# Attention in a two-layer hybrid block: maxima streamed one pair per step in fp16, sums by full-width matmuls, shift rows by DMA

## The reference

```python
s = jnp.einsum('bqhgd,bkhd->bhgqk', qi, k, preferred_element_type=F32) * scale
p = jax.nn.softmax(s, axis=-1).astype(v.dtype)
return jnp.einsum('bhgqk,bkhv->bqhgv', p, v)
```

## Time and profile before

| what | value |
|---|---|
| time, median of 3 runs | 4570.11 us (4565.5 to 4571.17) |
| time of the profiled execution | 4556.52 us, span 4554.7 us |
| TensorE busy | 3887.8 us, 85% of the span |
| VectorE, ScalarE, GpSimd busy | 2159.6, 1203.1, 798.9 us |
| maxima, VectorE L1465 | 600 instructions, 336.5 us busy, 327.8 us idle ahead of them |
| GpSimd adds L1414 and L1409 | 219 instructions, 450.6 and 63.4 us |

### The profile page before, as it was taken

How to read it: one execution, slowest core, us unless ns; L and a number is a source line. 1 busy time by engine, 2 the same in 40 slices (tenths; PEclk the granted TensorE clock), 3 DMA queues, 4 the chain that set the end, 5 groups by cost and what they waited for, 6 DMA issues and landing times. The chain is left out here.

```text
span 4554.7 us, 49366 instructions
## 1 busy us (share of the span) xinstructions
PE 3887.8 (85%) x20550; PEld 2092.8 (46%) x20550; DVE 2159.6 (47%) x3601; ACT 1203.1 (26%) x1589; POOL 798.9 (18%) x412
## 2 busy tenths in 40 slices
PE   6698459689989799999996696478799985999996
PEld 6455337323345555555553454455233332444443
DVE  1782886554530623333335683854555316333334
ACT  0321333223331321111112321332233323221211
POOL 0000641056650000000000000700277600000000
PEclk7898665689999799999998897755799997999998
DMA  4210013010002221111101210031100021111110
GB/s 167 54 38 4 1 44 116 17 35 9 1 3 81 74 65 42 42 39 40 42 28 37 56 41 1 1 123 54 30 8 1 1 74 46 51 51 51 51 47 37
DMA packets 207632, 194.37 MB, mean 43 GB/s; under 512 B 9719, under 2 KB 174386, under 8 KB 206770
## 3 DMA queue, kind: packets, MB, share of 16 engines
q1 hardware_dynamic: 203250, 182.84, 12.9%
q10 hardware_dynamic: 4160, 8.39, 0.5%
HBM read 167.48 MB, written 14.68 MB: 40 GB/s over the span
## 5 line engine op out<-in xcount | busy, mean ns | idle before, releaser
L324 PE MATMUL mlp_acc<-hh,mlp_w 128*128 128x512 f16 (+1 forms) x3840 | 752.8, 359 | 49.9 <-DVE mlp_w L314 49.9
L324 PE MATMUL mlp_acc<-mlp_aa,mlp_w 128*128 128x512 f16 (+1 forms) x3840 | 749.2, 358 | 0.0
L324 PEld LDWEIGHTS mlp_acc<-hh,mlp_w 128*128 128x128 f16 x3840 | 376.5, 98 | 424.3 <-DVE mlp_w L314 50.8
L324 PEld LDWEIGHTS mlp_acc<-mlp_aa,mlp_w 128*128 128x128 f16 x3840 | 375.8, 98 | 371.1
L1465 DVE TENSOR_REDUCE at_mx<-at_small 128x1 f32<-128x512 f32 (+1 forms) x600 | 336.5, 591 | 327.8 <-PE at_small L1511 197.1
L1414 POOL TENSOR_TENSOR at_accp<-at_accp,at_p 128x1024 f32<-128x1024 f32 x192 | 450.6, 2347 | 151.7 <-ACT at_p L1445 150.5
L324 PE MATMUL in_acc<-hh,in_w 128*128 128x512 f16 (+1 forms) x2088 | 400.2, 354 | 71.0 <-DVE in_w L314 58.5
L1445 ACT ACTIVATE at_p<-at_sT 128x1024 f32<-128x1024 f32 x246 | 252.1, 1025 | 475.9 <-PE at_sT L1556 458.3
L647 DVE SCALAR_TENSOR_TENSOR yf<-mlp_acc,yf 128x1280 f32<-128x1280 f32 (+1 forms) x112 | 152.0, 1357 | 398.6 <-PE mlp_acc L324 398.6
L324 PEld LDWEIGHTS in_acc<-hh,in_w 128*128 128x128 f16 (+1 forms) x2088 | 208.0, 100 | 261.3 <-DVE in_w L314 59.3
L634 DVE TENSOR_TENSOR mlp_r<-mlp_r 128x1280 f32<-128x1280 f32 (+1 forms) x64 | 86.9, 1358 | 476.2 <-ACT mlp_r L615 476.2
(11 more groups left out here) (268 smaller groups left out, 4870.2 us busy)
## 6 DMA issues: line engine op xcount, KB each, us to landing
mlp_stage<-in_w_ff SPq DMA_DIRECT2D x128, 512.0 KB, 3.9
pa_wada<-in_w_ada SPq DMA_DIRECT2D x16, 2048.0 KB, 8.2
in_stage<-in_w_in SPq DMA_DIRECT2D x36, 512.0 KB, 4.2
set_wada<-in_w_ada ACTq DMA_DIRECT2D x4, 2048.0 KB, 20.2
out_stage<-in_w_out SPq DMA_DIRECT2D x16, 512.0 KB, 5.0
nf_wada<-in_w_ada SPq DMA_DIRECT2D x4, 2048.0 KB, 8.7
x<-x_scratch SPq DMA_DIRECT2D x1, 5120.0 KB, 16.0
xin<-in_x SPq DMA_DIRECT2D x8, 512.0 KB, 6.1
```

The source lines that it names most:

```text
L324: last = self.nc.tensor.matmul(acc[0:mw, a:a + c], w[:, wh, k, m0:m0 + mw], src[:, sh, k0 + k, a:a + c], start=(k == 0 and wh == 0 and sh ...
```

## The change

MSHIFT is gone. Six things change:

- `plan()` spreads the maxima: one pair of tasks a step, ending LEAD=4 steps before their unit. The last chunk of 256 keys is taken for two query tiles in one task, so a long unit has 20 max tasks, all 512 wide; a short one has 4. They and the row task are all ahead of the values product.
- VectorE writes the maxima over chunks as fp16 into `top`; no negation follows.
- row: one fp16 product of `top` (8 columns) with an fp16 identity, which VectorE makes at the start. ScalarE copies 8x128 with scale -1 into `row`, and SyncE sends it by DMA into the queries, two DMAs for a long unit and four for a short one, behind the loads of the first three pairs of heads in its list.
- sum: two fp32 products, 64 columns of ones as the weights and 512 columns of `accp` moving, behind the values product. All 64 partitions of a par get the sum. ScalarE copies the 128x512 into `o32`.
- VectorE takes the reciprocal of `o32` itself, four pieces of 128x128, one a step, 5 to 8 steps after the unit's last, and the product with `acc` at 9. Where a short unit follows, all is done at step 4 after the last.
- PRING is 5, not 4. The bc task is gone.

```diff
-PRING = 4
+PRING = 5
+LEAD = 4
 def maxes(u):
+        if not units[u].long:
+            return [("max", u, par, 0, (q, q + 1)) for q in (0, 2) for par in range(2)]
+        whole = [("max", u, par, c, (q,)) for q in range(4) for c in range(2) for par in range(2)]
+        return whole + [("max", u, par, 2, (q, q + 1)) for q in (0, 2) for par in range(2)]
 def plan():
+        both = [(u, k) for u in range(1, U) for k in range(len(maxes(u)) // 2)]
+        when = {}
+        for n in range(len(both) - 1, -1, -1):
+            u, k = both[n]
+            when[n] = min(base[u] - LEAD, when.get(n + 1, N) - (1 if n + 1 < len(both) else 0))
+        for n, (u, k) in enumerate(both):
+            want.setdefault(max(when[n], n // 2), []).extend(maxes(u)[2 * k:2 * k + 2])
+        for u in range(1, U):
+            want.setdefault(base[u] - LEAD + 1, []).append(("row", u))
         for u in range(U):
             end = base[u + 1] - 1
             soon = u + 1 < U and not units[u + 1].long
+            sum_at[u] = min(end + (3 if soon else 4), N)
+            want.setdefault(sum_at[u], []).append(("sum", u))
+            for k in range(4):
+                piece_at.setdefault(min(end + (4 if soon else 5 + k), N), []).append((u, k))
+            scale_at[u] = min(end + (4 if soon else 9), N)
 # SyncE
+                for pr in range(QRING):
+                    load(pr)
+                for u in range(U):
+                    sp.wait_ge(s_row, u + 1)
+                    for par in range(2):
+                        for pr, tok, c, n in units[u].parts:
+                            r = 4 * par + c // P
+                            dst = shift_row(pr, par)[:, tok:tok + n]
+                            sp.dma_start(dst, row[r:r + n // P, u % 2, :]).then_inc(s_shift[u % 2], 16)
 # ScalarE
-                                nc.scalar.activation(row[:, tok:tok + n], sm[j % 2][R:R + 1, c:c + n], ACT.Copy)\
+                            nc.scalar.activation(row[:, u % 2, :], sm[j % 2][0:8, 0:P], ACT.Copy, scale=-1.0).then_inc(s_row, 1)
+                            nc.scalar.activation(o32[:, u % 2, :], sm[j % 2][:, :], ACT.Copy).then_inc(s_sums, 1)
 # VectorE
-                                ch(nc.vector.reduce_max(neg[:, u, :, :], mx[:, u, :, :, 0:len(cks)], AX.X))
-                                nc.vector.tensor_scalar(neg[:, u, :, :], neg[:, u, :, :], -1.0, MSHIFT,
+                                nc.vector.reduce_max(top[:, u, :].rearrange("p (a q) -> p a q", a=2),
+                                                     mx[:, u, :, :, 0:len(units[u].keys)], AX.X).then_inc(s_top, 1)
+                        part = o32[:, u % 2, k * P:(k + 1) * P]
+                        pieces[u] = ch(nc.vector.reciprocal(part, part))
 # TensorE
-                                last = nc.tensor.matmul(out[R:R + 1, q * P:(q + 1) * P], neg[:, u, par, q:q + 1],
+                            last = nc.tensor.matmul(out[0:8, 0:P], top[:, u, :], ident[:, :], start=True, stop=True)
-                                                            accp[:, u % 2, par, q * P:(q + 1) * P], e.ones[:, 0:1],
+                                last = nc.tensor.matmul(out[64 * par:64 * par + 64, :], e.ones[:, 0:64],
+                                                        accp[:, u % 2, par, :], start=True, stop=True)
-                                                            rc[:, u % 2, 4 * par + q:4 * par + q + 1].broadcast_to([P, 64]),
                     scores(i)
-                    tasks(i, slice(0, EARLY))
+                    tasks(i, ahead)
                     if i >= LAG:
                         weighted(i - LAG)
-                    tasks(i, slice(EARLY, None))
+                    tasks(i, ("sum",))
```

More of the change, by code:

```diff
@@ L1203 @@
 LAG = 2
-EARLY = 2
-PRING = 4
+PRING = 5
+LEAD = 4
 QRING = 3
@@ L1260, in maxes @@
     def maxes(u):
-        return [("max", u, par, q, c) for q in range(4) for c in range(len(units[u].keys)) for par in range(2)]
+        if not units[u].long:
+            return [("max", u, par, 0, (q, q + 1)) for q in (0, 2) for par in range(2)]
+        whole = [("max", u, par, c, (q,)) for q in range(4) for c in range(2) for par in range(2)]
+        return whole + [("max", u, par, 2, (q, q + 1)) for q in (0, 2) for par in range(2)]
+    sum_at, piece_at, scale_at = {}, {}, {}
     def plan():
         want = {}
[L1265 to L1273, removed]
+        for t in maxes(0) + [("row", 0)]:
+            want.setdefault(-1, []).append(t)
+        both = [(u, k) for u in range(1, U) for k in range(len(maxes(u)) // 2)]
[7 more added lines that the diff above has]
+            want.setdefault(base[u] - LEAD + 1, []).append(("row", u))
         for u in range(U):
@@ L1276, in plan @@
             soon = u + 1 < U and not units[u + 1].long
[L1277 to L1280, removed]
+            sum_at[u] = min(end + (3 if soon else 4), N)
[3 more added lines that the diff above has]
+            scale_at[u] = min(end + (4 if soon else 9), N)
         for i in sorted(want):
             for t in want[i]:
-                put(min(i, N), t)
+                put(i, t)
     plan()
@@ L1324, in attention, with shifts @@
                 last_max[t[1]] = kinds[:j + 1].count("max")
-            elif t[0] == "row":
-                rows_at[j] = sum(len(units[w[1]].parts) for w in small[:j + 1] if w[0] == "row")
-                rows_through[t[1]] = rows_at[j]
+        def shifts(u):
+            return sum(16 * 2 * len(units[v].parts) for v in range(u % 2, u + 1, 2))
         def hi_of(t, q):
@@ L1376, in place, with load @@
                     sp.dma_start(to, src).then_inc(signal, 16)
-                for pr in range(4):
+                def load(pr):
                     if pr % 2 == 0:
@@ new lines, in tasks @@
+                            for n, q in enumerate(tiles):
+                                pr, tok = units[u].tile(q)
+                                if pr < 4 and pr % 2 == 0 and pr not in loaded:
+                                    pe.wait_ge(s_kload[pr // 2], 16 * 6)
+                                    loaded.add(pr)
+                                if pr < 4:
+                                    R = slice(64 * par, 64 * par + 64)
+                                    query, key = hi_of(f.aq[R, pr, :], tok), kk[R, pr // 2, a:a + w]
+                                else:
+                                    b = 2 * (pr - 4) + par
+                                    query, key = f.qb[0:96, 0, b, tok:tok + P], f.kb[0:96, 0, b, a:a + w]
+                                last = nc.tensor.matmul(out[:, n * w:(n + 1) * w], query, key, start=True, stop=True)
+                        elif kind == "row":
+                            pe.wait_ge(s_top, u + 1)
+                            if u == 0:
+                                pe.wait_ge(s_id, 1)
+                            last = nc.tensor.matmul(out[0:8, 0:P], top[:, u, :], ident[:, :], start=True, stop=True)
+                        else:
@@ L1546, in scores @@
                     if s == 0:
-                        pe.wait_ge(s_row, rows_through[u])
+                        pe.wait_ge(s_shift[u % 2], shifts(u))
+                        for pr, _, _, _ in units[u].parts:
+                            if pr < 4 and (pr, "q") not in loaded:
+                                pe.wait_ge(s_load[pr % QRING], per_pair * (pr // QRING + 1))
+                                loaded.add((pr, "q"))
                     if i >= 2:
```

117 lines of the change are left out of this document (45 added, 72 removed).

## The result

| | before | after |
|---|---|---|
| median of 4 runs each on one chip | 4570.64 us (4565.5 to 4576.94) | 4463.71 us (4456.26 to 4468.1) |
| ratio, 95% interval | | 0.9764 (0.9745 to 0.9783) |
| profiled execution: time, span | 4556.52, 4554.7 us | 4466.4, 4464.6 us |

The forecast was 4484 with a range of 4445 to 4530. In the profiled pair the gain is 90.1 us. Counted from the first load of keys to the end of GpSimd's last low half, attention takes 753.8 us in place of 855.3: 101.5 less. The code outside attention, which is the same, takes 11.4 us more. For that reason I compare kernels by their medians and, for sizes, by their attention alone.

A forecast was written before the change was run, and what follows sets the result against it. TensorE's list was taken to bound the kernel. Loops of 353.3 us (from 399.1) and 325.1 (from 374.3) gave -95.0; starts +8.7 and -1.2, ends +2: -85.5, so 4484 against the median; range 4445 to 4530.

The forecast's parts named there:

- What bounds it: Both attention stretches: TensorE's list, busy in 99%, sets the pace; GpSimd's adds start every 2.42 us and stay under it.
- A step with a pair of maxima: TensorE in attention: a pair adds 0.32 us to a bare 1.98 in group A, 0.43 to 2.42 in group B.
- The sum: Two full-width fp32 products on TensorE, once a unit: 1.12 us, being 1.02 and 0.1 for the change of tasks.
- The row: Row's fp16 product on TensorE, mostly waiting for a max's bank: 1.3 us a unit in group A, 0.8 in B.
- The long waits: Layer 0, long units behind short ones: the values product waits 3.7 us for acc's bank; two of them, 7.4.
- The start at the lower clock: Start of each layer's attention loop: 5 us for running at the lower clock, as before.
- The first row: Start of attention: row DMAs behind SyncE's loads delay the first scores by 8.7 us in layer 0; -1.2 in layer 1.
- The tails: Ends of the layers: bare reciprocal pieces against the sums and spreads they replace, +2 us for both layers.
- The waits are hidden: Rival: waits for row and acc hidden, group A's unit 24.3 us in place of 25.5; 4452 us, chance 0.17.
- The clock falls still: Rival: waits of the new order make the clock fall, 28 us of the saving come back; 4512 us, chance 0.13.
- Rows late: Rival: the row's DMA lands 3 to 4 us later, 25 unit starts wait 1 to 2 each; 4522 us, chance 0.06.
- The reciprocals shut out: Rival: VectorE's reciprocal pieces wait for GpSimd's adds; 4682 us, chance 0.05, or 4566 with 1 us waits, chance 0.05.

The follow-up runs named there:

- e4: Changed kernel with PRING 4 in place of 5: 4471.79 us, ratio to the kernel before 0.9781.
- e6: Changed kernel with the row task behind the values product of its step, not ahead of it: 4453.87 us, ratio to the kernel before 0.9735.
- e7: Changed kernel with e5's and e6's edits, plus sum, reciprocals and product by acc one step earlier ahead of a short unit: 4442.14 us.
- e5: Changed kernel with the first unit's row DMAs ahead of the third pair's loads in SyncE's list: 4456.47 us, ratio to the kernel before 0.9745.
- e1: Changed kernel with the old sums: eight one-column fp32 products, small reciprocal, eight spreading products, copy and product by VectorE: 4529.17 us.
- e8: Kernel before with only the new sums: two full-width fp32 products, ScalarE copy, four reciprocals and product by VectorE, no spread: 4502.09 us.
- e10: Changed kernel with a tensor_scalar by 1.0 behind each of a unit's four reciprocals, on the same SBUF piece: 4511.56 us, ratio to the kernel before 0.9869.
- e2: Changed kernel with the old burst of 24 max tasks in a unit's first 8 steps and the row at step 8: 4475.53 us.

## Why the prediction was right

The mechanism held in its steps, and what was off were sizes, most of them a little too high and two too low. The forecast of 85.5 us of attention was 16 short of the 101.5 measured; that the terms were off in both directions helped it. One by one:

- **What bounds it.** TensorE's list, before and after. Nothing else became the bound: with GpSimd's adds at 2351 ns a step of 2.31 was kept with four buffers too (e4).
- **A step with a pair of maxima**, bare 1.98 + 0.32: 2.30 forecast, 2.31 measured; in group B 2.85 forecast and measured.
- **The sum**, 1.12 forecast, 0.85 measured. I took 1.02 and added 0.1 for the change of tasks. The sum starts 0.91 behind the values product, where scores start 1.02 behind it, and the next scores 0.97 behind the sum, so it costs 0.91 + 0.97 - 1.02 = 0.86. 24 sums between the exponentials make -6.5 us.
- **The row**, 1.3 forecast for group A, 1.00 measured; in group B 0.8 and 0.79. The 1.17 us between the pair and the third task, read in the earlier trace rows, came again to the hundredth. I had put more on it for a VectorE that is late; it isn't. 16 rows make -4.8 us. Three of the nine rows of group B stand in a step without maxima and cost 0.15 alone, another -1.9. e6 shows that it is a wait and not work.
- **The long waits**, 3.7 each and two of them: the values product stood 3.24 and 2.49 us, less than that, but the clock fell behind both. The units took 31.75 - 24.94 = 6.8 and 35.2 - 30.14 = 5.1 us more than their neighbours; a second sum lies in each, which the forecast counts with the sums, so 5.9 and 4.2 are the waits with what follows, 10.1 in place of 7.4. This size was off the other way, +2.7. That the wait brings the fall is read from the order in time. e7 bears it out in part: with the shorter waits of 1.76 and 0.58 us there is one fall in place of two.
- **The start at the lower clock**, 5 forecast. The first three steps took 4.34, 4.35 and 6.09 us in place of 2.31, which is 7.9 more, and 7.7 in layer 1: +5.6.
- **The steps counted.** From the first to the last exponential there is one step fewer than there are steps, and I summed all of them: -2.4 in each layer.
- **The first row.** +8.7 forecast in layer 0, 35.64 - 27.35 = 8.3 measured; in layer 1 -1.2 forecast, 25.0 - 26.12 = -1.1. e5 gives the cause: with the DMAs ahead of the third pair's loads it is gone.
- **The tails**, +2 forecast, -2.4 measured: 14.41 and 11.57 us for 15.33 and 13.06. The bare pieces start 0.83 apart, eight in 6.63 us. From the first of the last sums to the last product with `acc` are 9.5 us in layer 0, where the sums and spreads of before took 10.8:

```profile
1310.15 6.63 DVE L1501 RECIPROCAL at_o<-at_o 128x128 f32<-128x128 f32 x8 [12.78 <-ACT at_o L1453]
```

The loops were forecast at 353.3 and 325.1 us and took 348.2 and 319.0. The terms above make -6.5 - 4.8 - 1.9 + 2.7 + 5.6 - 4.8 = -9.7 of that -11.2. The remaining 1.5 us I didn't trace. With the loops at -11.2, the tails at -4.4 and the starts at -0.3, attention gained 101.5 in place of 85.5. In the medians it is 107, since the rest of the program moves too.

**The rivals.** "The waits are hidden": no, both are in the trace, the row's in each unit and `acc`'s twice. Hidden they are worth 18.4 us (e6) and 3.5 (e7 against e6, first to last exponential), 22 in all, where I had put 32; e7 leaves a wait of 1.76. Its time, 4452, is nearer to the median than mine, but for another reason, the sizes above. "The clock falls still": in part, behind the two long waits and at the starts, nowhere in a steady unit. One of my reasons against it was wrong: the new waits are not all shorter than the old ones, 3.24 and 2.49 us against 1.6 at most. e1 shows that with the products of one column it falls there, and e8 that without them it doesn't. But they aren't the only thing that does it: e10 has none, and the clock falls behind waits of 1.54 us. "Rows late": no; with two steps in place of three they are 0.4 us late (e2). "The reciprocals shut out": no (e10).

## What to carry to other kernels

Cost a product by what moves through the array: eight products of a few columns against full weights held TensorE for 2 us, two full ones for 1, and the clock fell behind some of the former (e1). A task that waits for a bank costs what is queued behind it, so put it behind the long product that doesn't need the bank; here this order alone was worth 18 us. A DMA that is small and urgent belongs ahead of the loads that aren't, and when work is moved off an engine, look at the one place where the schedule is irregular (here the short units): waits of 3.24 and 2.49 us there cost 5.9 and 4.2, the rest being the clock that fell behind them.

## What the runs showed of the hardware that I had not expected

- A cast by VectorE of 128 columns, fp32 to fp16, took 2.27 us beside GpSimd's memset of 2.22, which only writes. It starts 0.04 us behind it and ends 0.08 behind it, in both layers of all ten kernels that have it, as the tensor_scalar of e10 ends behind an add. No run has this cast by itself; the tensor_scalar of as many columns took 0.23 when nothing stood in its way. It is hidden here. In order of time, kernel after, start of layer 1:

```profile
3189.19 2.22 POOL L1418 MEMSET at_ks<- 1x2560 f16 x1 [73.53 <-POOLq L1053]
3189.23 2.27 DVE L1509 CAST at_ident<-ident 128x128 f16<-128x128 f32 x1 [0.32 <-PEq L1053]
```

- A wait of 3.24 us in TensorE, after 100 us at full clock, was followed by some 5 us of work at the lower level. Shorter waits can do it too: one of 1.76 us in e7, and 8 of 12 of 1.54 in e10. The waits ahead of the old maxima, up to 1.6 us, did no such harm by themselves: e8 keeps them and has no fall in a steady unit, while e1, with the one-column products and without those waits, has five. No run here says what tells the one kind of wait from the other.
- A DMA of a row, SBUF to SBUF, is usable soon: in layer 0 the two of unit 0 are issued from 953.38 to 954.73, and the scores that wait for them start at 955.79.

```profile
955.79 0.61 PE L1572 MATMUL at_sT<-at_qq,at_kk 128*128 128x512 f16 x1 [13.40 <-DMA at_qs<-at_row]
```

- The same code outside attention took 3696 to 3719 us over twelve profiles, and its first stretch, ahead of attention, 912 to 926.
